# Attention weighted a key block at a time over up to 512 queries, with one store a head

## What is computed

```
s = q @ k.T + bias, masked to keys not after the query
p = softmax(s)            # stick attention: exp of scores and a reversed running sum instead
out = p @ v
```

## Time and profile before

| | |
|---|---|
| median of 3 runs | 3614.53 us (3612.91 to 3617.69) |
| profiled execution, own time | 3612.36 us |
| its span | 3610.2 us |
| TensorE (PE) busy | 3376.2 us, 94% |
| weight loads (PEld) busy | 2676.6 us, 74% |
| VectorE (DVE) busy | 1536.0 us, 43% |
| ScalarE (ACT) busy | 1267.9 us, 35% |
| granted TensorE clock, mean | 0.959 |

### The profile page before, as it was taken

The page is one execution under the profiler, slowest core; times in us unless marked ns, Lnnn a source line. Parts: engine busy times, 40 slices in busy tenths (PEclk is TensorE's granted clock), DMA queues, the critical chain, the costliest instruction groups (busy, mean ns, idle before and its releaser), DMA issues. The chain is left out here.

```text
span 3610.2 us, 37765 instructions
## 1 busy us (share of the span) xinstructions
PE 3376.2 (94%) x15040; PEld 2676.6 (74%) x15040; DVE 1536.0 (43%) x2407; ACT 1267.9 (35%) x2181; POOL 329.6 (9%) x160
## 2 busy tenths in 40 slices
PE   7988889999999999999788999999999988889998
PEld 6755668877888888877476788878887756668886
DVE  4142431125333333435676633343334448763334
ACT  2324542223232322232466422232223235643222
POOL 0310214430000000013100000000000420000000
PEclk9988979999999999999799999999999979999999
DMA  3210213322333333332000233323333310023332
GB/s 132 82 41 24 71 35 100 99 88 88 100 94 99 97 96 93 99 105 74 30 1 23 83 96 97 97 85 96 97 94 102 94 41 7 1 76 94 99 97 73
DMA packets 76783, 279.58 MB, mean 77 GB/s; under 512 B 8768, under 2 KB 9024, under 8 KB 76352
## 3 DMA queue, kind: packets, MB, share of 16 engines
q1 hardware_dynamic: 76608, 277.16, 25.5%
HBM read 275.03 MB, written 2.10 MB: 77 GB/s over the span
## 5 line engine op out<-in xcount | busy, mean ns | idle before, releaser
L516 ACT ACTIVATE w_hi<-raw_slabs 128x1024 fp32r<-128x1024 f32 x496 | 524.6, 1058 | 1296.1 <-PE ps L556 1178.8
L531 DVE TENSOR_TENSOR w_lo<-raw_slabs,w_hi 128x1024 fp32r<-128x1024 f32 x372 | 455.1, 1224 | 748.9 <-ACT w_hi L516 748.8
L556 PE MATMUL ps<-in_hi,w_hi 128*128 128x512 f32 x1904 | 744.9, 391 | 8.2 <-DVE in_lo L836 8.0
L556 PE MATMUL ps<-in_hi,w_lo 128*128 128x512 f32 x1904 | 742.7, 390 | 0.0
L556 PE MATMUL ps<-in_lo,w_hi 128*128 128x512 f32 x1904 | 742.4, 390 | 0.0
L556 PE MATMUL ps<-parts,w_hi 128*128 128x512 f32 x2304 | 712.7, 391 | 7.7 <-PEq L380 7.7
L531 POOL TENSOR_TENSOR w_lo<-raw_slabs,w_hi 128x1024 fp32r<-128x1024 f32 x124 | 312.2, 2519 | 2532.4 <-ACT w_hi L516 2532.2
L556 PEld LDWEIGHTS ps<-parts,w_hi 128*128 128x128 f32 x2304 | 433.5, 188 | 99.3 <-issue 10.0
L556 PE MATMUL ps<-parts,w_lo 128*128 128x512 f32 x1152 | 449.2, 390 | 0.0
L556 PEld LDWEIGHTS ps<-in_hi,w_hi 128*128 128x128 f32 x1904 | 358.1, 188 | 89.8 <-issue 8.9
L556 PEld LDWEIGHTS ps<-in_hi,w_lo 128*128 128x128 f32 x1904 | 358.1, 188 | 74.3
(11 more groups left out here) (259 smaller groups left out, 3514.5 us busy)
## 6 DMA issues: line engine op xcount, KB each, us to landing
raw_slabs<-weights SPq DMA_DIRECT2D x508, 512.0 KB, 3.6
big<-rope SPq DMA_DIRECT2D x2, 2304.0 KB, 9.3
x_resid<-xT SPq DMA_DIRECT2D x8, 256.0 KB, 4.4
outT<-x_resid SPq DMA_DIRECT2D x8, 256.0 KB, 2.0
const_cols<-consts SPq DMA_DIRECT2D x1, 836.0 KB, 9.1
scratch<-brow SPq DMA_DIRECT2D x1, 768.0 KB, 9.9
vector_cols<-vec SPq DMA_DIRECT2D x2, 45.5 KB, 9.7
vector_cols<-vec SPq DMA_DIRECT2D x1, 69.0 KB, 2.8
```

The source lines that it names most:

```text
L516: self.nc.scalar.activation(self.w_hi[:, m % SPLIT, :], self.raw[:, n % RAW, :], ACT.Copy)\
L531: (self.nc.gpsimd if i is None else self.nc.vector).tensor_tensor(self.w_lo[:, m % SPLIT, :], self.raw[:, n % RAW, :], self.w_hi[:, m % SP ...
L556: mm = k.nc.tensor.matmul(out, lhsT, rhs, start=(c == 0 and m == 0), stop=(last and m == 2))
```

## The change

A *branch* is now the four units of one head (and one of the sparse stage's three branches) with query blocks 0 to 3, and the list of the sparse stage is written in this order: for each head four compressed units, four selected, four window ones. The turned probabilities of a branch are collected in four rows of scratch, row j holding key block j over 512 queries (`turned_in`). `weigh` runs once a branch, behind the unit with the last query block (`closes`): key block j is weighed over the queries P*j to 512, since earlier queries don't see it. The output of a head is one bank of 512 columns, stored once. Two sets of rows alternate between branches, and two banks between heads. The ring of probabilities goes from 6 to 4 buffers, to make room; the stick stage puts its rows into `big`.

```diff
-    def __init__(self, scores, width, values, group, first, last, rows, out, mask, scale=1.0, gate=None):
+    def __init__(self, scores, width, values, qb, head, first, last, rows, out, mask, scale=1.0, gate=None):
         self.scores, self.width, self.values = scores, width, values
-        self.group, self.first, self.last, self.rows, self.out = group, first, last, rows, out
+        self.qb, self.head, self.first, self.last, self.rows, self.out = qb, head, first, last, rows, out
         self.scale, self.mask, self.gate = scale, mask, gate
         self.blocks = [(a, min(P, width - a)) for a in range(0, width, P)]
+        self.closes = qb == QB - 1
...
+def turned_in(k, u, rows_of, bank):
+    w, n = u.blocks[0][1], len(u.blocks)
+    return (rows_of(u.branch % 2)[0:w, 0:n, P * u.qb:P * u.qb + P],
+            k.ps[0:w, bank, 0:P * n].rearrange("p (t n) -> p t n", n=P))
 def weigh(k, u, pt, bank):
-    for j, ((a, w), val) in enumerate(zip(u.blocks, u.values)):
-        mm = k.nc.tensor.matmul(k.ps[:, bank, 0:P], val, pt[0:w, a:a + P], start=(u.first and j == 0),
+    for j, ((_, w), val) in enumerate(zip(u.blocks, u.values)):
+        mm = k.nc.tensor.matmul(k.ps[:, bank, P * j:T], val, pt[0:w, j, P * j:T], start=(u.first and j == 0),
                                 stop=(u.last and j == len(u.blocks) - 1))
     return mm
-def attend(k, pe, u, n, units, probs, ready, turned, laid, unit_done, stored):
...
-    if 0 <= u - 2 < n:
+    if 0 <= u - 2 < n and units[u - 2].closes:
         one = units[u - 2]
         pe.wait_ge(laid, k.at(laid, u - 1))
-        if one.first and one.group >= 3:
-            pe.wait_ge(stored, k.at(stored, one.group - 2))
-        weigh(k, one, k.scr[:, 6 + (u - 2) % 3, :], 5 + one.group % 3).then_inc(unit_done, 1)
-def lay_and_store(k, act, u, n, units, turned, laid, unit_done, stored):
+        if one.first and one.head >= 2:
+            pe.wait_ge(stored, k.at(stored, one.head - 1))
+        weigh(k, one, rows_of(one.branch % 2), 5 + one.head % 2).then_inc(branch_done, 1)
+def lay_and_store(k, act, u, n, units, rows_of, turned, laid, branch_done, stored):
     nc = k.nc
     if 0 <= u < n:
+        one = units[u]
         act.wait_ge(turned, k.at(turned, u + 1))
-        if u >= 3:
-            act.wait_ge(unit_done, k.at(unit_done, u - 2))
-        rows = units[u].blocks[0][1]
-        cols = P * len(units[u].blocks)
-        nc.scalar.activation(k.scr[0:rows, 6 + u % 3, 0:cols], k.ps[0:rows, 3 + u % 2, 0:cols], ACT.Copy)\
-            .then_inc(laid, 1)
-    if 0 <= u - 3 < n and units[u - 3].last:
+        if one.qb == 0 and one.branch >= 2:
+            act.wait_ge(branch_done, k.at(branch_done, one.branch - 1))
+        to, turned_bank = turned_in(k, one, rows_of, 3 + u % 2)
+        nc.scalar.activation(to, turned_bank, ACT.Copy).then_inc(laid, 1)
+    if 0 <= u - 3 < n and units[u - 3].closes and units[u - 3].last:
         one = units[u - 3]
         lo, hi = one.rows
-        act.wait_ge(unit_done, k.at(unit_done, u - 2))
-        nc.scalar.activation(one.out, k.ps[lo:hi, 5 + one.group % 3, 0:P], ACT.Copy).then_inc(stored, 1)
+        act.wait_ge(branch_done, k.at(branch_done, one.branch + 1))
+        nc.scalar.activation(one.out, k.ps[lo:hi, 5 + one.head % 2, :], ACT.Copy).then_inc(stored, 1)
+def number_branches(units):
+    assert all(u.qb == i % QB for i, u in enumerate(units))
+    for i, u in enumerate(units):
+        u.branch = i // QB
+    return sum(1 for u in units if u.closes and u.last)
...
     n = len(units)
-    ring, lag = 6, 3
+    ring, lag = 4, 3
     probs = lambda i: k.scr[:, i % ring, :]
+    rows_of = lambda n: k.scr[:, ring + QB * n:ring + QB * (n + 1), :]
+    heads = number_branches(units)
...
-def stick_phase(k, units, index, steps):
...
     bank = lambda i: k.ps[:, i % 4, 0:units[i].width]
-    turn_bank, out_bank = lambda i: 4 + i % 2, lambda i: 6 + i % 2
-    soft_at, rest_at, laid_at, probs = [lambda i, b=b: k.scr[:, b + i % 3, :] for b in (0, 3, 6, 9)]
+    turn_bank, out_bank = lambda i: 4 + i % 2, lambda i: 6 + units[i].head % 2
+    soft_at, rest_at, probs = [lambda i, b=b: k.scr[:, b + i % 3, :] for b in (0, 3, 6)]
+    heads = number_branches(units)
...
-                if 0 <= i - 4 < n:
+                if 0 <= i - 4 < n and units[i - 4].closes:
                     u = i - 4
+                    one = units[u]
                     pe.wait_ge(laid, k.at(laid, u + 1))
-                    if u >= 2:
-                        pe.wait_ge(stored, k.at(stored, u - 1))
-                    weigh(k, units[u], laid_at(u), out_bank(u)).then_inc(unit_done, 1)
+                    if one.head >= 2:
+                        pe.wait_ge(stored, k.at(stored, one.head - 1))
+                    weigh(k, one, rows_of(one.branch % 2), out_bank(u)).then_inc(branch_done, 1)
...
-                if 0 <= i - 5 < n:
+                if 0 <= i - 5 < n and units[i - 5].closes:
                     u = i - 5
                     lo, hi = units[u].rows
-                    act.wait_ge(unit_done, k.at(unit_done, u + 1))
-                    nc.scalar.activation(units[u].out, k.ps[lo:hi, out_bank(u), 0:P], ACT.Copy).then_inc(stored, 1)
+                    act.wait_ge(branch_done, k.at(branch_done, units[u].branch + 1))
+                    nc.scalar.activation(units[u].out, k.ps[lo:hi, out_bank(u), :], ACT.Copy).then_inc(stored, 1)
...
                 if 0 <= i - 3 < n:
                     u = i - 3
-                    cols = units[u].width
+                    one = units[u]
                     dve.wait_ge(turned, k.at(turned, u + 1))
-                    if u >= 3:
-                        dve.wait_ge(unit_done, k.at(unit_done, u - 2))
-                    nc.vector.tensor_copy(laid_at(u)[:, 0:cols], k.ps[:, turn_bank(u), 0:cols]).then_inc(laid, 1)
-    k.passed(scored=n, soft=2 * n, logged=n, broken=n, rest=n, exponent=n, probs_ready=n, turned=n, laid=n, unit_done=n,
-             stored=n, top8=len(steps), top8_taken=len(steps), select_made=rows_done(steps))
+                    if one.qb == 0 and one.branch >= 2:
+                        dve.wait_ge(branch_done, k.at(branch_done, one.branch - 1))
+                    to, turned_bank = turned_in(k, one, rows_of, turn_bank(u))
+                    nc.vector.tensor_copy(to, turned_bank).then_inc(laid, 1)
...
             w = P * (qb + 1)
             pairs = [(q(h)[:, P * qb:P * qb + P], key(h)[:, 0:w])] + (extra(h, w) if extra else [])
             lo = 64 * (h % 2) if dims == 64 else 0
-            units.append(Unit(pairs, w, [v(kb, h) for kb in range(qb + 1)], QB * h + qb, True, True,
-                              (lo, lo + dims), out(h)[lo:lo + dims, P * qb:P * qb + P], masks(qb), scale))
+            units.append(Unit(pairs, w, [v(kb, h) for kb in range(qb + 1)], qb, h, True, True,
+                              (lo, lo + dims), out(h)[lo:lo + dims, :], masks(qb), scale))
     return units
     units = []
     for h in range(HEADS):
         lo = 64 * (h % 2)
+        more = dict(head=h, rows=(lo, lo + 64), out=ys(1)(h)[lo:lo + 64, :])
+        qs = lambda qb: two_heads(14)(h)[:, P * qb:P * qb + P]
+        gate = lambda qb, b: gates[:, qb, 4 * b + h:4 * b + h + 1]
         for qb in range(QB):
-            wd = P * (qb + 1)
-            more = dict(group=QB * h + qb, rows=(lo, lo + 64), out=ys(1)(h)[lo:lo + 64, P * qb:P * qb + P])
-            gate = lambda b: gates[:, qb, 4 * b + h:4 * b + h + 1]
-            qs = two_heads(14)(h)[:, P * qb:P * qb + P]
-            units.append(Unit([(qs, kc[h % 2])], wide, [vc], first=True, last=False, gate=gate(0),
+            units.append(Unit([(qs(qb), kc[h % 2])], wide, [vc], qb, first=True, last=False, gate=gate(qb, 0),
                               mask=k.mask("cmp_neg")[:, wide * qb:wide * (qb + 1)], **more))
-            for b, (kt, col) in enumerate(((ks, VS0), (kw, VW0))):
-                units.append(Unit([(qs, one_half(kt)(h)[:, 0:wd])], wd, [shared(col)(kb, h) for kb in range(qb + 1)],
-                                  first=False, last=(b == 1), gate=gate(b + 1), mask=causal(qb), **more))
+        for b, (kt, col) in enumerate(((ks, VS0), (kw, VW0))):
+            for qb in range(QB):
+                wd = P * (qb + 1)
+                units.append(Unit([(qs(qb), one_half(kt)(h)[:, 0:wd])], wd, [shared(col)(kb, h) for kb in range(qb + 1)],
+                                  qb, first=False, last=(b == 1), gate=gate(qb, b + 1), mask=causal(qb), **more))
...
-    stick_phase(k, units, select, range(TOP_CUTS[2], TOP_STEPS * (QB - 1)))
+    stick_phase(k, units, lambda n: big[:, 25 + QB * n:25 + QB * (n + 1), :], select, range(TOP_CUTS[2], TOP_STEPS * (QB - 1)))
```

19 lines of the change are left out of this document (11 added, 8 removed).

## The result

The changed kernel takes 3642.59 us (median of 4 runs, 3637.93 to 3643.04) beside 3615.74 us for the kernel before (4 runs, 3612.91 to 3617.69): a ratio of 1.0071, with a 95% interval of 1.0055 to 1.0087. That is 26.9 us slower; the forecast was 8.5 us and its range ended at 3632. The profiled execution took 3643.04 us, its span 3641.3 us.

The account below looks back on a forecast made before the run. TensorE was taken to bound forgetting, selected and, closely, sparse attention, VectorE MLA and stick. Selected +1.6, MLA +3.0, sparse 0.0, stick +0.4 and forgetting +3.3 gave +8.3 on 3614.5: 3623 us, range 3612 to 3632.

Parts of the forecast that it names:

- three signs named for a wrong prediction: Sparse stage below 65 us, a 512-column weighing's pitch well under 0.43 us, or a last burst at the lower clock.
- a saving of 3.9 us of TensorE's work a sparse stage: Sparse stage: 3.4 us from fewer changes to 32 rows, 0.1 from fewer records, 0.4 from 8 causal branches.
- rival 3: Weighings: loads are exposed, a wide record costs its 0.19 us load instead of 0.43; 31 us less, 3584; chance 0.02.
- The +2.0: Start of the sparse stage: TensorE idles about 2.9 us before the first weighing at step 8, against 0.85 before.
- +0.9: Sparse stage, later steps: VectorE lags by 1.25 us, of which 0.3 us was charged on each of three heads.
- +0.35: MLA, middle: a 2.17 us burst holds back the next score, and VectorE's lag covers all but 0.35 us.
- My timetable: MLA heads 2 and 3 laid out with these durations; VectorE up to two units behind covers all but 0.35 us.
- 0.98 a stage: End of a stage: +0.65 us waiting for the last head's copy and +0.33 for the 512-column store, nothing covering either.
- 0.17 more in MLA: End of MLA: 0.17 us more weighing left behind the last turn, 20 records instead of 18.
- +2.5: Forgetting stage: the clock rises only in the first burst, costing 1.7 to 3.4 us; 2.5 taken.
- +0.2 each: Stick, two stages: -0.8 us as the last turn no longer follows a weighing, then +0.98 for the end.
- Rival 2: Ends of MLA, sparse and stick: last bursts run at 1.2 GHz, 2.1 us more each, +21, 3635; chance 0.10.

Follow-up runs that it names:

- the light VectorE: Top-8 steps beside attention cut to 8 columns, in the kernel before and in the changed kernel: 3588.58 and 3605.89 us, a single run each.

## Why the prediction was wrong

The direction was right, and the size was not: 8.5 us forecast, 26.9 measured, and the stage that the forecast had at nothing, sparse, lost most. Of the three signs named for a wrong prediction one appeared, and once only: the last burst of the second stick stage was run at the lower clock. The sparse stage didn't fall below 65 us, and the pitch of wide weighings didn't change. In short: a saving of 3.9 us of TensorE's work a sparse stage was entered as time and bought about a tenth of that; the bursts cost more than forecast, since turns then wait for ScalarE's copies; and stick lost some 7 us together with a lower clock. Point by point.

**Pitches and counts: right.** A causal burst takes 2.16 us, as forecast. The 32-row weighing of 512 columns has its successor 1.06 us behind it, 0.20 us over two pitches of 0.43, so a change to 32 rows and back costs what it did with 128 columns (there the rows give 0.42 less 0.22; the prediction read 0.41). Loads are not exposed (rival 3), 368 records are left.

**The value of a saving in the sparse stage: the step that failed.** "With 0.4 for 8 causal branches a sparse stage has 3.9 us less of TensorE work" was entered as time, -3.9 in the sum, because TensorE was busy for 16.24 of 16.46 us in a head. The work did go away, but leaving out 6.0 us of TensorE's work bought 0.6 of time (in the old order). At that rate, an estimate, the term was worth -0.4, and 3.5 us a stage, 7 of the 18 that are missing, are this. A window of a middle head is full also when work only fills it. Why it only fills it is in part argued: VectorE had 14.87 of the same 16.46 us, and if each step is as long as the slower of the two, a step in which VectorE is late gets nothing from a shorter TensorE. The waits that took the saved time were for VectorE's scaling and for ScalarE's copies in equal parts (4.0 and 4.3 us), and no run left work out with a light VectorE.

**The start of the sparse stage: wrong in kind.** The +2.0 was for TensorE idle ahead of step 8. Its waits for VectorE's scaling up to there are 1.1 us in the changed kernel (0.3 at 1827.11 and 0.9 at 1831.18) and were 0.8. What came instead is the lower clock, 3.4 us of it.

**The burst in the middle: too small.** For the sparse stage the forecast had +0.9 ("of the 1.25 us I put 0.3 on each of three heads"); for MLA +0.35; for selected 0. Spreading the blocks gives back 4.3 and 3.5 us of the changed kernel's sparse stage, and the widening of the compressed weighing alone is paid to the hundredth. In selected the middle costs 1.0, and it is the wait for the copy: the third turned bank removes 1.0 there and 1.0 to 1.2 in sparse. My timetable left this wait out. turn(u) needs the bank of unit u-2, whose copy on ScalarE is queued behind a later exponential. Before, a weighing stood between one turn and the next; when it is moved away nothing covers that time. I asked what would be late next of the last turn of a stage only.

**The ends: right in MLA, a little small elsewhere.** Forecast 0.98 a stage, and 0.17 more in MLA; the last turn to the next stage is +1.22 in MLA, and the last head at the old pace gives back 1.1 to 1.3 in MLA, selected and forgetting. In selected the last burst waited 1.10 us for its copy, and not 0.7: ScalarE was still at the 512-column store of the head before, which the forecast had called free. In sparse the end is 0.7.

```profile
1969.30 0.58 ACT L1683 ACTIVATE act<-ps 64x512 f32<-64x512 f32 x1
...
1970.42 2.42 PE L1648 MATMUL ps<-scratch,big 128*128 128x512 f32 x8 [1.10 <-ACT scratch L1678]
```

**The clock: a fitting number in one stage, missed in others.** In the forgetting stage I took +2.5 from a rise near 329 or 333; it came at 333, 7 us later than before, and the stage took +4.2. That is no proof of the mechanism that I gave, a rise held back until the first burst. The same instructions take 50.55 us in one execution and 53.73 or 53.72 in others (the ring of four, the light VectorE), by a clock that rises 7 to 8 us later without any burst; those with one store a head take 50.85 in one and 54.02 and 55.22 in others (new order; three weighings left out). So the change may cost this stage up to 4.2 us or, next to 55.22, nothing. At least its end is real: the last head at the old pace is 1.3 shorter. For the medians the share of this stage stays open; that the changed kernel had 54.77, 54.82 and 54.73 in three profiles, and the one with spread blocks 64.05, speaks for some effect of the edits on the clock, and no run isolates it.

In stick the forecast had +0.2 each and priced the lower clock only for the last burst. In the first layer that burst ran at full speed and stretches before it did not; in the second it ran mostly at the lower clock, 1.6 us longer:

```profile
1941.74 2.42 PE L1648 MATMUL ps<-big 128*128 128x512 f32 x8 [0.78 <-DVE big L1855]
...
3156.69 4.02 PE L1648 MATMUL ps<-big 128*128 128x512 f32 x8 [0.78 <-DVE big L1855]
```

The changed stick code ran in four kernels, in two layers each, and its times stand in the order of the mean clock: 46.33 us at 0.96, 47.5 to 48.4 at 0.93 (three stages), 49.85 to 49.91 at 0.90 (four). These last four are the ones whose last burst ran at the lower clock, in 4.02 to 4.64 us; in the others it took 2.42. The old weighings there gave 45.05 to 45.10 at 1.00, 46.2 to 46.4 at 0.96, and 45.6 to 46.6 at 0.93. At 0.96 the two are equal, by the one changed stage that ran so, and with no low stretch at all (the light VectorE) it was 41.48 against 41.69. The low stretches are 3.4 us longer in the first layer and 10.2 in the second than they were; at half speed that is up to 1.7 and 5.1 us lost, of +2.1 and +4.8. So the change by itself seems to cost stick next to nothing, as forecast, and the +6.9 us go with the clock. This is a reading of times side by side, not an experiment, and the mean clock is not the whole of it: at 0.93 the changed stages are 0.9 us or more longer than the old ones. What in the bursts lowers the clock was not tried by itself. Rival 2 was right for the second stick stage (its price was 2.1 to 2.3 us, 1.6 is what it took) and for none of the other last bursts, which all took 2.42 us. At the start of the sparse stage 3.4 us are run at the lower clock, up to 1.7 us lost; in the two kernels with the new list and narrow weighings some 14 us are low, and the list costs 5.0.

**The sum by measured prices.** Sparse 2 x (-0.4 for the saving, +3.9 for the bursts, +0.7 for the end) = +8.4; MLA 2 x (1.1 for the end, 0.45 for the bursts that spreading gave back) = +3.1 of 4.3, the rest not attributed; selected 2 x (1.2 + 1.0) = +4.4; stick +6.9; forgetting +1.0 (next to 53.7) to +4.2. That is 24 to 27 us, of 29.3 measured in these stages. It is put together afterwards, with stick and forgetting entered as they were measured, and shows no more than that the terms have the right size. Not separated is how much of the bursts' price in the sparse stage is VectorE left idle behind a late score and how much goes with the order of the list: no kernel had bursts of the causal branches in the old order, for which the scratch rows don't suffice.
